# Recurrence of a hybrid block: where one weight transfer, one group of outputs and half of a shift stand in a turn

## The reference

```python
def centred_token_shift(p, mu):
    pad = jnp.pad(p, ((0, 0), (1, 1), (0, 0)))
    return p + mu * (0.5 * (pad[:, :-2] + pad[:, 2:]) - p)

def step(state, inp):                       # per head, 64 x 64 state
    r_t, w_t, k_t, v_t, kk_t, kka_t = inp
    sa = einsum('bhvk,bhk->bhv', state, kk_t)
    state = state * w_t[:, :, None, :] - sa[..., None] * kka_t[:, :, None, :] + v_t[..., None] * k_t[:, :, None, :]
    return state, einsum('bhvk,bhk->bhv', state, r_t)

y = y_f + y_b                               # forward and reversed scan
y = normalised per head(y) * ln_w + ln_b
out = (y + bonus) * gate                    # bonus = sum(r * (k_f + k_b) * r_k) * v
```

## Time and profile before

| what | value |
|---|---|
| median of 3 runs | 4038.08 us (4036.07 to 4041.71) |
| the profiled execution's own time | 4031.3 us |
| its span | 4029.6 us |
| TensorE busy | 3569.6 us, 89% of the span |
| VectorE busy | 1871.4 us, 46% |
| GpSimd busy | 1115.8 us, 28% |
| ScalarE busy | 684.5 us, 17% |
| mean granted TensorE clock | 0.985 of full speed |

### The profile page before, as it was taken

How to read it: one execution, slowest core, us unless ns; L and a number is a source line. 1 busy time by engine, 2 the same in 40 slices (tenths; PEclk the granted TensorE clock), 3 DMA queues, 4 the chain that set the end, 5 groups by cost and what they waited for, 6 DMA issues and landing times. The chain is left out here.

```text
span 4029.6 us, 73073 instructions
## 1 busy us (share of the span) xinstructions
PE 3569.6 (89%) x31239; PEld 2158.7 (54%) x31239; DVE 1871.4 (46%) x3194; ACT 684.5 (17%) x1240; POOL 1115.8 (28%) x1734
## 2 busy tenths in 40 slices
PE   7989999999999879999999999989977777777776
PEld 3456666656665546666678888556423222222222
DVE  1334544544554347677670000036565564655644
ACT  2223223222322211212220000010110100100101
POOL 2044334334433400100000000004444444444432
PEclk9999999999999989999999999999999999999999
DMA  9322222222322237466653444529999999999997
GB/s 381 110 56 74 59 70 65 67 66 56 81 57 66 56 119 239 150 191 191 202 168 147 167 154 159 198 94 426 404 427 427 427 428 427 428 428 427 428 427 321
DMA packets 466529, 893.46 MB, mean 222 GB/s; under 512 B 84524, under 2 KB 302270, under 8 KB 396990
## 3 DMA queue, kind: packets, MB, share of 16 engines
q0 software_dynamic: 73728, 536.90, 31.7%
q1 hardware_dynamic: 300800, 305.80, 23.1%
q10 hardware_dynamic: 91710, 46.43, 4.0%
HBM read 876.46 MB, written 12.62 MB: 221 GB/s over the span
## 5 line engine op out<-in xcount | busy, mean ns | idle before, releaser
L2563 PE MATMUL ps<-w_slots,diag 128*128 128x512 f32 x1920 | 883.4, 605 | 273.2 <-DMA w_slots<-in_peer_v,ixv 239.8
L2563 PEld LDWEIGHTS ps<-w_slots,diag 128*128 128x128 f32 x1920 | 349.6, 191 | 805.1 <-issue 444.8
L985 PE MATMUL ps<-hT,w_slots 128*128 128x512 f32 (+1 forms) x1536 | 628.6, 542 | 19.7 <-ACT r_s L749 16.9
L1657 PE MATMUL ps<-hT,w_slots 128*128 128x256 f32 (+1 forms) x1504 | 499.8, 486 | 6.4 <-PEq L655 4.9
L2176 POOL DMA_INDIRECT w_slots<-in_peer_v,ixv x244 | 258.0, 1057 | 612.7 <-PE ps L2563 524.7
L2340 DVE SCALAR_TENSOR_TENSOR junk<-w_slots,hT 128x2048 f32<-128x2048 f32 x128 | 293.5, 2293 | 271.5 <-DMA w_slots<-in_peer_u,ixu 271.3
L2340 DVE SCALAR_TENSOR_TENSOR junk<-ybT,hT 128x2048 f32<-128x2048 f32 x128 | 293.4, 2293 | 261.5 <-DMA ybT<-in_peer_u,ixu 261.2
L985 PEld LDWEIGHTS ps<-hT,w_slots 128*128 128x128 f32 x1536 | 272.8, 191 | 193.9 <-issue 169.2
L1657 PEld LDWEIGHTS ps<-hT,w_slots 128*128 128x128 f32 x1504 | 281.6, 190 | 173.6 <-issue 153.0
L724 POOL TENSOR_TENSOR Ypart<-Ym,Sm 128x126 f32<-128x126 f32 (+22 forms) x496 | 187.2, 377 | 535.2 <-DMA Sm<-s_blocks 497.6
L862 DVE SCALAR_TENSOR_TENSOR w_slots<-ps,em,w_slots 128x64 f32<-128x64 f32 x448 | 106.5, 280 | 321.0 <-PE ps L1054 321.0
(11 more groups left out here) (383 smaller groups left out, 4479.1 us busy)
## 6 DMA issues: line engine op xcount, KB each, us to landing
w_slots<-in_w_mod SPq DMA_DIRECT2D x128, 512.0 KB, 4.8
w_slots<-in_w_in SPq DMA_DIRECT2D x56, 1024.0 KB, 5.7
w_slots<-in_w_in ACTq DMA_DIRECT2D x44, 1024.0 KB, 6.5
w_mod_ring<-in_w_mod SPq DMA_DIRECT2D x16, 2048.0 KB, 13.6
w_slots<-in_w_in SPq DMA_DIRECT2D x7, 4096.0 KB, 12.9
w_slots<-in_w_branch_a SPq DMA_DIRECT2D x4, 4096.0 KB, 13.6
w_slots<-in_w_branch_b SPq DMA_DIRECT2D x4, 4096.0 KB, 13.4
w_slots<-in_w_out SPq DMA_DIRECT2D x4, 4096.0 KB, 12.9
```

Source lines behind the costliest of these rows:

```text
L985: last = mm(ps[:, 4, t0:TOK], w[m % 2][:, k, :], hT[:, k, t0:TOK], start=(k == 0), stop=(k == KC - 1))
L1657: last = mm(out, w[m % SLOTS_W][:, k, :], hT[:, k, t0:TOK], start=(k == 0), stop=(k == KC - 1))
L2563: last = nc.tensor.matmul(ps[:, 4 * n + c, :], diag[:, k % 2, :], vb[k % NB][:, c * 512:(c + 1) * 512], start=False, stop=False)
```

## The change

Three moves, none of which adds or removes an instruction other than semaphore waits:

1. SyncE issues the transfer of pair p's receptance weights not at the end of the turn before, but in turn p - 1 behind the load of `Sm`.
2. TensorE computes `outputs(1)` between the receptance piece and the value piece instead of before the receptance piece's last twelve steps. The mean follows behind the first four steps of the values. On ScalarE the square root of the key norm and the receptance's two copies come ahead of the copy of the outputs.
3. VectorE does the value shift in two parts with the third step of the chain between them.

```diff
@@ SyncE
                             sp.dma_start(Sm[...], s_dram...).then_inc(s_in, 16)
+                    if 0 < a_ < PAIRS:
+                        reload(a_, 1)
                     if a_ + 1 < PAIRS:
                         sp.wait_ge(*PA.by("a1", a_))
...
                         sp.dma_start(ya_dram[:, z, :], ot[:, z % 2, :]).then_inc(ya_out[z % 2], 16)
-                    if a_ + 1 < PAIRS:
-                        reload(a_ + 1, 1)
@@ ScalarE
-                    if Z:
-                        act.wait_ge(*PD.by("y", z))
-                        need(act, VD, "yc", z - 1)
-                        copy(y[...], ps[:, 0:4, 0:2 * CH]..., AD.did("yf"))
                     if A:
                         act.wait_ge(*PA.by("kss", p))
                         nc.scalar.activation(rn[:, :], ps[:, 5, :], ACT.Sqrt).then_inc(*AA.did("norm"))
...
                         padded("r", p, 1, r_s[:, :])
+                    if Z:
+                        act.wait_ge(*PD.by("y", z))
+                        need(act, VD, "yc", z - 1)
+                        copy(y[...], ps[:, 0:4, 0:2 * CH]..., AD.did("yf"))
@@ VectorE
                     chain(2, z)
                     if B:
-                        shift(1, i, 0, v_s[:, :])
+                        shift_before(1, i, 0, v_s[:, :])
+                    chain(3, z)
+                    if B:
+                        shift_behind(1, i, 0, v_s[:, :])
                         dve.wait_ge(*PA.by("bonus", i))
                         dve.wait_ge(*VA.by("sh1b", i))
                         tt(bonus[...], ps[:, 7, 0:SEQ], v_s[:, SEQ:TOK], ALU.mult).then_inc(*VA.did("bv"))
-                    for j in range(3, NC - 2):
+                    for j in range(4, NC - 2):
                         chain(j, z)
@@ TensorE
                         sums(1, p)
+                    piece("r", 4, KC)
                     if Z:
                         outputs(1, z, i)
-                    piece("r", 4, 12)
+                    piece("v", 0, 4)
                     if Z:
                         pe.wait_ge(*VD.by(f"c{NC - 2}_1", z))
                         pe.wait_ge(*AD.by("yf", z))
                         mm(ps[:, 6, 0:SEQ], head_mean[:, :], y[:, :], start=True, stop=True).then_inc(*PD.did("mean"))
-                    piece("r", 12, KC)
-                    piece("v", 0, 4)
                     if B:
                         solved(0, i)
```

More of the change, by code:

```diff
@@ L817, in _ @@
                         exps(1, p)
-                    if Z:
-                        act.wait_ge(*PD.by("y", z))
-                        need(act, VD, "yc", z - 1)
-                        copy(y[:, :].rearrange("p (n r t) -> p r n t", n=2, r=4), ps[:, 0:4, 0:2 * CH].rearrange("p r (n t) -> p r n t", n=2), AD.did("yf"))
                     if A:
@@ L827, in _ @@
                         padded("r", p, 1, r_s[:, :])
+                    if Z:
+                        act.wait_ge(*PD.by("y", z))
+                        need(act, VD, "yc", z - 1)
+                        copy(y[:, :].rearrange("p (n r t) -> p r n t", n=2, r=4), ps[:, 0:4, 0:2 * CH].rearrange("p r (n t) -> p r n t", n=2), AD.did("yf"))
                     if B:
@@ L846, in _, with shift_before, shift_behind, shift @@
                 tt, stt = nc.vector.tensor_tensor, nc.vector.scalar_tensor_tensor
-                def shift(n, p, s0, out):
-                    s = out.rearrange("p (s t) -> p s t", t=SEQ)
-                    half = shifts[:, p, 2 * n + 1:2 * n + 2]
+                def shift_before(n, p, s0, out):
+                    s, half = out.rearrange("p (s t) -> p s t", t=SEQ), shifts[:, p, 2 * n + 1:2 * n + 2]
                     dve.wait_ge(*AA.by(f"keep{n}", p))
                     stt(s, pad[:, n, s0:2, 0:SEQ], half, s, ALU.mult, ALU.add).then_inc(*VA.did(f"sh{n}a"))
+                def shift_behind(n, p, s0, out):
+                    s, half = out.rearrange("p (s t) -> p s t", t=SEQ), shifts[:, p, 2 * n + 1:2 * n + 2]
                     dve.wait_ge(*VA.by(f"sh{n}a", p))
                     stt(s, pad[:, n, s0:2, 2:SEQ + 2], half, s, ALU.mult, ALU.add).then_inc(*VA.did(f"sh{n}b"))
+                def shift(n, p, s0, out):
+                    shift_before(n, p, s0, out)
+                    shift_behind(n, p, s0, out)
                 def chain(j, z):
```

## The result

The changed kernel takes 3981.6 us in the median of 4 runs (3974.5 to 3987.1), the kernel before 4039.5 us (4036.1 to 4041.7). The ratio is 0.9856, with a 95% interval of 0.9839 to 0.9874: 58 us faster, where 38.6 were forecast.

What follows compares the result with a forecast made beforehand. The prediction took TensorE's work plus its gaps in the recurrence as the bound. Its terms, 14.8 + 6.7 + 17.1 = 38.6 us, brought the median of 4038.1 us to 3999.5 us, range 3987 to 4020 us.

Steps and rivals of the forecast that it cites:

- What bounds the kernel: In the recurrence, TensorE's own work plus its gaps, 70 us over the stretch; other engines' savings count only by closing gaps.
- Part 1: Outputs moved between receptance and values fill TensorE's 1.06 us wait for `r_s` in 14 turns: 14.8 us.
- The mean's late place: Mean directly before `solved`, its copy covered by four value steps: cost nothing, at most one copy, 0.47 us.
- Part 2: Value shift split around VectorE's third chain update, so TensorE's wait before chain steps goes: 6.7 us.
- wait for `bv`: Before TensorE turns `Ah`: `bv` ends later but in time; costed at nothing, up to 0.5 us a turn otherwise.
- Part 3: Receptance weights' 1 MB transfer moved away from the Gram groups, where it delays TensorE's instructions: 17.1 us.
- the additions' level: Gram groups' gaps in 15 turns would fall from 25.4 us to the 8.3 us lost in the additions.
- all 25.4: Upper bound for moving the receptance weights: every Gram gap of 15 turns goes, giving 3991.2 us.
- a sum of 38.6: Total forecast saving on TensorE's path: 14.8 + 6.7 + 17.1 us.
- The rule from the Trainium skill: Instruction fetch is hidden by dispatch, so moving the weights brings nothing: 21.5 us saved, 4016.6 us; rival's chance 0.2.
- The slack: After the savings, 0.9 us stays before `solved` and 0.2 us before the additions, so TensorE is nearly caught by VectorE.
- Slower through `Sm`: Weights behind the load of `Sm` hold it up, delaying GpSimd and `Yt`; up to 4082 us, chance 0.04.

Runs made afterwards that it cites:

- late_store: Changed kernel with the 128 KB results store moved from beside the additions to behind the load of `Sm` in the next turn: 3979.8 us, ratio 0.9853.
- keys_late: Changed kernel with the next pair's keys asked for when the additions are done, instead of directly behind the load of `Yt`: 3984.2 us, ratio 0.9863.
- ahead_of_sm: Changed kernel with the receptance weights asked for directly ahead of the load of `Sm` instead of behind it: 3995.1 us, ratio 0.9889.
- ab_late: Changed kernel with both stores of the blocks behind the second mask, so no transfer runs beside the moved turns' Gram groups: 3986.8 us, ratio 0.9866.

## Why the prediction was wrong, point by point

- **What bounds the kernel**, TensorE's gaps at three places of a turn: right. All three closed or shrank, and the time went with them.
- **Part 1**, 14.8 us for the wait on `r_s`: the wait fell by that (16.9 to 2.0). Its "96 small matmuls" are 96 records, 48 matmuls, which changes nothing. The term missed 3.7 us of TensorE's busy time in the receptance. The mean's late place, costed at nothing, cost nothing: 838.63, with `solved` straight behind it.
- **Part 2**, 6.7 us: right, 7.4 alone, and no wait for `bv` appeared.
- **Part 3**, 17.1 us, is the step that failed, in two ways. "So I take the Gram groups down to the additions' level" was a wrong analogy: the gaps fell by 22.4 us (28.7 to 6.3), near the upper bound of 25.4, because the additions have gaps of their own that no transfer causes (late_store, keys_late). And the bound itself, "all 25.4", left out the clock: 7.7 us in the profile (10.6 to 2.9). It could be read before the result. I took the gaps from the rows of idle time and never looked at what came right behind them; at 901.66 the row with 3.18 us in place of 1.98 stood in the trace. The part measures 34 us alone, in which the interval reaches from 27 to 40. The mechanism itself, instructions that come late behind the transfer, was right.
- **The idle time** shrank by 40.7 us against a sum of 38.6. That is partly luck: the Gram groups gave 5.3 us more than their term, and 4.3 us of longer waits in turn 0 and the transitions, which no term had, took most of it back.
- **The rule from the Trainium skill** ("Runtime: NRT & Kernel Launch", "Instruction fetch mechanics", fetch hidden by the dispatch rate) would have given 4016.6 us. Here the gaps follow the traffic at 28.9, 17.5 and 6.3 us for a whole, a half and no transfer, and every stop of 0.3 us and more ends 1.0 to 1.65 us after an instruction packet: the rule doesn't hold for matmuls this small.
- **The slack**: the additions' 0.2 us fits what came. In the turn shown VectorE comes to its step behind the transitions without any idle time (846.93), and TensorE waited for it once in 15 turns, 0.4 us. `solved` waits only in turn 0, where it already did: 7.2 us after 4.9.
- **Slower through `Sm`**: it didn't come, as argued from `Yt`'s landing; ahead_of_sm shows that the place behind the load is what spares it.

The profile's recurrence adds up: Gram gaps -22.4, clock -7.7, `r_s` -14.9, chain -6.7, receptance steps -3.7, additions -1.0, against +2.0 in the transitions and +2.3 in turn 0, is -52.1 of 52.2 us. That the medians differ by 58 and not by 50 is not settled: the profile before is 8.2 us below its median, and the number of clock drops differs between profiles with the same gaps (2 to 9, up to 12 us), so it may be their number in the other runs, which have no trace.

```profile
846.93 2.28 DVE L952 TENSOR_TENSOR w_slots<-ps,id 128x2048 f32<-128x2048 f32 x1
```

## What to carry to other kernels

When an engine stops with no semaphore to blame, look at what the DMA engines do in those microseconds, and ask for large transfers while the engine runs long instructions, not while it goes through hundreds of short ones. A gap on TensorE can have two prices, its own length and what the granted clock does behind it: look at the rows directly after the gap before pricing its removal. And take an analogy for what will remain only from a place whose gaps have the same cause.

## What the runs showed that I had not expected

- A gap of about 2 us between Gram matmuls was followed in some turns, not in all, by about 3.5 us at a granted clock of 0.50, worth 1.7 us each: 2 to 9 times in the 15 turns of the five profiles with the whole transfer, never in the other nine, where half of it or nothing runs beside the Gram groups at that place. It isn't gone for good: in the last turn, where 1 MB runs beside the Gram groups, the changed kernel's gaps of 3.34 and 1.69 us each have one behind them. The length of the gap doesn't decide alone: in late_store, keys_late and ahead_of_sm one such drop each came behind a gap of 0.6 to 0.7 us in the outputs of turn 14, the changed kernel had none behind its gap of 0.58 us at the same place, and in the kernel before none came behind the 2.43 us of the earlier trace rows.
- 1 MB beside some 250 records of small matmuls costs 1.5 us of gaps a turn and half of it 0.75: (28.7 - 6.3) / 15 and (17.5 - 6.3) / 15.
- Gaps of about 0.5 us a turn stay in the additions, and 0.4 to 0.9 us in single Gram groups (ab_late), with no data transfer in flight. They too end 1.0 to 1.65 us after an instruction packet. Why it comes late there is open.
- The gap of a turn mostly stands ahead of the same matmul in every kernel, whatever the time: 1.61 us in the changed kernel (792.15) and 2.43 us in the kernel before (823.51) both have 7 records of the second Gram group left.
